# Two pads of 8 bytes in a partition, one ahead of the weight ring and one behind the arena

## The chip, the cores and the metric

The kernel runs on one core of one Trainium2 chip. The metric is the time on the device in microseconds for one execution. The kernel before takes 3476.79 us, the median of three runs (3474.61 to 3479.54).

## What is computed

Two stacks of two layers each work on one sequence of 256 tokens of width 1024, all in float32. The first stack has, in each layer, a feed-forward, a mixer and a feed-forward; the mixer is a bidirectional state-space mixer in layer 0 and multi-head latent attention in layer 1. The second stack has a recurrent mixer with pooling and a feed-forward that picks 16 of 16,384 experts per head. Nearly all of the time goes to matrix products with weights:

```python
h = modulate(x, norm_g[i, 0], mod[:, 0, 0], mod[:, 0, 1])
x = x + FFN_RES_WEIGHT * mod[:, 0, 2][:, None, :] * swiglu(h, w_gate, w_up, w_down)
...
act = jax.nn.gelu(jnp.einsum('td,ted->te', hx, u_sel), approximate=False)
return jnp.einsum('te,ted->td', gx * act, v_sel)
```

The kernel computes the expert layer densely: it multiplies with all rows of `peer_u` and `peer_v` and weights the result with gates that are zero for the experts that were not picked.

## The kernel before

**Tiling.** Activations stand transposed, 128 features in the partitions and 256 tokens in the free dimension. Weights come from memory as 957 blocks of 128 x 1024 float32 (512 KB, 4,096 bytes in each partition), in the order in which they are used. A block is used as eight 128x128 stationary operands.

**Weights in two parts.** For most stages each block is split. ScalarE rounds it into one of the four slots of `weights_hi` (`split_hi`, L1146), VectorE subtracts that from the block and writes the rest (`split_lo`, L1641), and TensorE makes three matmuls for each 128x128 piece: rounded weights with the rounded and with the remaining part of the activations, and the rest of the weights with the rounded part of the activations. `columns_in_parts` (L517) does this for a product that streams all eight feature tiles of `hh` and `h` (24 matmuls into one region of PSUM). `rows_in_parts` (L550) does it for a product that streams one tile, whose rounded part is in `small` and whose rest is in `work` (three matmuls into each of eight regions). `front` (L529, L530, L543) does it for the first three blocks of a stage. L504 opens accumulators with 512-column matmuls of zeros. L896 makes 128x128 float32 transposes.

**Where data stands.** The blocks go to a ring of 4 slots (`ring`) and, in some stages, to 8 more slots inside the arena, whose rest part is written in place under the name `more_lo`. The arena is 128 KB in a partition; every stage lays its own temporaries in it. Modulation weights go from a queue of GpSimd to four further places of the arena and are multiplied and summed there by VectorE (L1569). The experts' activations go to memory from `small` (`rs`, `rv`) and come back to `work`.

**Odd offsets in the arena before.** The convolution of the state-space mixer (L1699) adds four shifted copies: step by step it writes `o[:, to]` with `to` from element 2, 1, 0 and 0 on, so 8, 4, 0 and 0 bytes past the tile's start; the first and the last have 254 elements, the middle two 255. In the recurrent mixer four rows of ZPAD are 257 elements apart, and L1870 reads `z[:, 1:257]` of row `p % 4`, which begins 4, 8, 12 and 0 bytes past a multiple of 16 for p = 0, 1, 2, 3.

**Order.** SyncE issues the blocks' transfers, each waiting until the block that last used its slot was used (`block_used`). TensorE waits for `block_lo`, VectorE for `block_hi`, ScalarE for the transfer and for the slot of `weights_hi`.

**Addresses.** The tensors are allocated one behind the other in a partition. The program of the kernel before has them at these bytes: `ring` 16,512; `weights_hi` 32,896; `arena` 49,280, with `more_lo` inside it at 80,000; `x` 180,352; `h` 188,544; `hh` 196,736; `vfirst` 204,928; `cols` 209,024 (2,648 bytes long); `kept` 211,680; `zeros` 213,728; `eps` 213,984 (80 bytes long); `modc` 214,080; `one_minus_k_a` 215,040; `work` 215,072 (its second half, with the rest part of the gated rows, 219,168); `small` 223,264. Four constants of 4 bytes or less stand ahead of the ring at 16,384, 16,416, 16,448 and 16,480. The partition has 229,376 bytes, and the last tensor ends at 228,640.

Of the kernel before, what the change touches and what calls it, by code (L numbers as in the profile page):

```python
# [16 lines left out]
P = 128  # L17
# [252 lines left out]
def build(nc, stream, mods, cols_d, consts_d, x_d, pos_d, wuq_d, wukv_d, cond_d, keys_d, pool_d, lora_d, gup_d, vup_d, acts_d, out_d):  # L270
    with ExitStack() as ctx:
        def sb(name, shape, dt=F32):
            return ctx.enter_context(nc.sbuf_tensor(name, shape, dt))
# [6 lines left out]
        def sb_twice(name, shape, parts):  # L280

            with nc.sbuf_tensor(name, shape, F32) as whole:
                pass
            return whole, [sb(f"{name}_{i}", p, dt) for i, (p, dt) in enumerate(parts)]

        ring, (ring_lo,) = sb_twice("ring", [P, RING, 1024], [([P, RING, 1024], F32R)])
        whi = sb("weights_hi", [P, WS, 1024], F32R)
        with nc.sbuf_tensor("arena", [P, 128, 256], F32) as AR:
# [1 line left out]
        sb("arena_low", [P, 30, 256])  # L290
        more_lo = sb("more_lo", [P, MORE, 1024], F32R)
        sb("arena_high", [P, 128 - 30 - 4 * MORE, 256])
        x = sb("x", [P, DT, T])

        h, (h_lo,) = sb_twice("h", [P, DT, T], [([P, DT, T], F32R)])
# [2118 lines left out]
```

## Time and profile before

| | |
|---|---|
| median of three runs | 3476.79 us (3474.61 to 3479.54) |
| span of the profiled execution | 3476.7 us |
| TensorE matmul busy / weight load busy | 96% / 92% |
| VectorE, ScalarE, GpSimd busy | 74%, 46%, 6% |
| TensorE's granted clock, mean | 0.987 of 2.4 GHz |
| DMA engines, mean busy share | 58%, 203 GB/s |

The page gives the busy time of each engine, the chain of work that ended last and the costliest groups of instructions. A group line names the source line, the engine, what is written from what, the shapes and the count; then the busy time and the mean of one in ns; then the idle time of the engine before them and what ended it. Matmuls overlap in the array, so the mean of one (some 280 ns) is a latency; how often one starts is read from pieces of the chain or from the timeline.

### The profile page before, as it was taken

To read this page: it belongs to the slowest core of one execution; us is meant where nothing else is said; L and a number is where in the kernel's file an instruction comes from. 1 tells how busy PE (TensorE), PEld (TensorE's weight loads), DVE (VectorE), ACT (ScalarE), POOL (GpSimd) and SP (SyncE) were. 2 spreads that over 40 slices of the span, in tenths; PEclk is the share of its full clock that TensorE was granted. 3 is DMA by queue.
4 is the path that set the end of the run, shared out by engine and by line. 5 is a ranking of instruction groups with operands and counts; after the bars stand their busy time and mean duration, and the time that the engine had idled before them with its cause. 6 is when DMAs were issued, how large, how long until landed. Compare 5 with 4: busy or idle time off the path is not lost.

```text
span 3476.7 us, 68787 instructions
## 1 busy us (share of the span) xinstructions
PE 3342.0 (96%) x26804; PEld 3203.1 (92%) x26804; DVE 2579.5 (74%) x4576; ACT 1608.5 (46%) x2594; POOL 198.7 (6%) x331
## 2 busy tenths in 40 slices
PE   6999989999999998999999999999899999999998
PEld 5999869999967998889999999998789999999998
DVE  7889667888736896746977867776755977777776
ACT  3456644454445445134444444444414445444444
POOL 1100001101000220200000000000300000000000
PEclk9999999999999999999999999999999999999999
DMA  9964218979613993034664466665215665456665
GB/s 369 359 221 169 74 49 324 336 261 334 249 46 113 385 374 127 31 132 171 228 207 169 166 225 229 230 229 174 75 46 171 230 221 175 169 203 229 232 228 181
DMA packets 246578, 707.46 MB, mean 203 GB/s; under 512 B 27472, under 2 KB 93008, under 8 KB 244928
## 3 DMA queue, kind: packets, MB, share of 16 engines
q1 hardware_dynamic: 212112, 571.64, 47.2%
q0 software_dynamic: 34224, 132.46, 10.2%
q8 instruction: 167, 2.74, 0.3%
q14 instruction: 75, 0.61, 0.1%
HBM read 669.40 MB, written 34.60 MB: 202 GB/s over the span
## 4 chain that ended last, share of the span: by engine, by line
PE 85%; DVE 7%; DMA 4%; ACT 2%; issue 2%; SPq 0%; POOL 0%; DVEq 0%; ACTq 0%; POOLq 0%
PE psum L517 39%; PE psum L550 26%; PE psum L1074 3%; DMA ring<-stream 2%; PE psum L896 2%; PE psum L1009 1%; PE psum L647 1%; DVE ring L1641 1%; PE psum L916 1%; PE psum L498 1%; PE psum L529 1%; DMA arena<-mod_weights 1%; PE psum L530 1%; DVE arena L1569 1%; ACT weights_hi L1146 1%
## 5 line engine op out<-in xcount | busy, mean ns | idle before, releaser
L517 PE MATMUL psum<-hh,weights_hi 128*128 128x256 f32 x4216 | 1212.2, 288 | 19.2 <-ACT arena L1360 8.1
L1146 ACT ACTIVATE weights_hi<-ring 128x1024 fp32r<-128x1024 f32 x711 | 752.0, 1058 | 993.6 <-DMA ring<-stream 928.6
L517 PE MATMUL psum<-h,weights_hi 128*128 128x256 f32 x4216 | 1197.5, 284 | 0.0
L1641 DVE TENSOR_TENSOR ring<-ring,weights_hi 128x1024 fp32r<-128x1024 f32 x711 | 870.1, 1226 | 440.0 <-ACT weights_hi L1146 434.9
L517 PE MATMUL psum<-hh,ring 128*128 128x256 f32 x2976 | 845.5, 284 | 0.0
L517 PEld LDWEIGHTS psum<-hh,weights_hi 128*128 128x128 f32 x4216 | 814.2, 193 | 26.8 <-issue 11.3
L517 PEld LDWEIGHTS psum<-h,weights_hi 128*128 128x128 f32 x4216 | 814.1, 193 | 0.3
L550 PE MATMUL psum<-small,weights_hi 128*128 128x256 f32 x2752 | 774.5, 281 | 4.9 <-DVE work L1665 3.3
L550 PE MATMUL psum<-work,weights_hi 128*128 128x256 f32 x2752 | 772.1, 281 | 0.0
L550 PE MATMUL psum<-small,ring 128*128 128x256 f32 x2304 | 646.1, 280 | 0.0
L517 PEld LDWEIGHTS psum<-hh,ring 128*128 128x128 f32 x2976 | 574.9, 193 | 0.0
L550 PEld LDWEIGHTS psum<-small,weights_hi 128*128 128x128 f32 x2752 | 518.9, 189 | 7.6 <-issue 5.3
L550 PEld LDWEIGHTS psum<-work,weights_hi 128*128 128x128 f32 x2752 | 519.0, 189 | 0.0
L550 PEld LDWEIGHTS psum<-small,ring 128*128 128x128 f32 x2304 | 434.0, 188 | 0.0
L517 PE MATMUL psum<-hh,more_lo 128*128 128x256 f32 x1240 | 351.5, 283 | 0.0
L1641 DVE TENSOR_TENSOR more_lo<-arena,weights_hi 128x1024 fp32r<-128x1024 f32 x214 | 261.1, 1223 | 75.2 <-ACT weights_hi L1146 72.3
L1569 DVE SCALAR_TENSOR_TENSOR arena<-arena 128x1024 f32<-128x1024 f32 x232 | 281.7, 1219 | 11.4 <-DMA arena<-mod_weights 11.1
L1146 ACT ACTIVATE weights_hi<-arena 128x1024 fp32r<-128x1024 f32 x214 | 225.0, 1053 | 114.3 <-PE psum L517 87.0
L517 PEld LDWEIGHTS psum<-hh,more_lo 128*128 128x128 f32 x1240 | 238.7, 193 | 0.0
L2101 DVE TENSOR_SCALAR work<-kept,small 128x128 f32<-128x128 f32 x512 | 142.6, 342 | 83.0 <-PE psum L1074 77.5
L2112 DVE TENSOR_TENSOR work<-work,arena 128x256 f32<-128x256 f32 x256 | 159.1, 623 | 0.0
L2183 POOL DMA_DIRECT2D arena<-mod_weights x208 | 109.8, 528 | 575.8 <-DVE arena L1569 572.3
(410 smaller groups left out, 3897.0 us busy)
## 6 DMA issues: line engine op xcount, KB each, us to landing
ring<-stream SPq DMA_DIRECT2D x735, 512.0 KB, 3.6
arena<-mod_weights POOLq DMA_DIRECT2D x224, 512.0 KB, 6.3
arena<-stream SPq DMA_DIRECT2D x222, 512.0 KB, 5.7
acts<-small SPq DMA_DIRECT2D x256, 128.0 KB, 2.2
work<-acts SPq DMA_DIRECT2D x256, 128.0 KB, 2.2
arena<-cond_rows POOLq DMA_DIRECT2D x3, 1024.0 KB, 7.6
arena<-w_uq POOLq DMA_DIRECT2D x1, 3072.0 KB, 10.3
arena<-constants POOLq DMA_DIRECT2D x2, 1200.0 KB, 5.7
```

The lines of the kernel that those rows point to most:

```text
L498: mm = pe.matmul(PS[:, 2, 0:T], ones, SQ[:, d, :], start=(d == 0), stop=(d == DT - 1))
L517: mm = pe.matmul(out, lhs[:, d, :], rhs[:, d, :], start=(d == 0 and p == 0), stop=(d == DT - 1 and p == 2))
L529: pe.matmul(out, w[:, d, :], h_hi[:, d, :], start=opens and d == 0, stop=False, skip_group_check=True)
L550: mm = pe.matmul(acc[:, d, :], lhs[:, d, :], rhs, start=False, stop=False, skip_group_check=True)
L896: mm = pe.matmul(PS[:, (4 * st + b) % 8, j * P:(j + 1) * P], lhs[:, c, :], rhs[:, c, :], start=True, stop=True)
L1074: mm = pe.matmul(PS[:, 4 + g % 4, j * P:(j + 1) * P], OHI[:, g % 2, j, :], OHJ[:, g % 2, j, :], start=True, stop=True)
L1146: act.activation(whi[:, NTH[n] % WS, :], raw(n), ACT.Copy).then_inc(sem["block_hi"], 1)
L1569: return dve.scalar_tensor_tensor(PRODUCT[:, m % 2, :], block, 1.0, COND[:, 0 if g < 6 else 1, :], ALU.mult, ALU.mult, accum_out=modc[:, g ...
L1641: dve.tensor_tensor(low(n), raw(n), whi[:, NTH[n] % WS, :].bitcast(F32), ALU.subtract)\
L2101: dve.tensor_scalar(OHI[:, g % 2, j, :], iota, ijg[:, 0, t:t + 1], ijg[:, 2, t:t + 1], ALU.is_equal, ALU.mult)
L2112: dve.tensor_tensor(gat[:, k % 4, :], sil[:, k % 4, :], WALL[:, :, i * 4 + k], ALU.mult).then_inc(sem["pe_gated"], 1)
L2183: pool.dma_start(MODRING[slot], mods[i * MOD_RING + (first + slot + MOD_RING)]).then_inc(mod_full[slot], 16)
```

## The change

Two tensors are allocated that nothing reads or writes: `line_half`, 8 bytes in a partition, ahead of the ring, and `line_rest`, 8 bytes, between the arena and `x`. The description of the change is that weight ring, rounded weights and arena begin 8 bytes past a multiple of 16 in a partition and everything else is where it was, modulo 16. No instruction is changed but for the addresses of its operands.

```diff
@@ -283,6 +283,7 @@
                 pass
             return whole, [sb(f"{name}_{i}", p, dt) for i, (p, dt) in enumerate(parts)]
 
+        sb("line_half", [P, 2])
         ring, (ring_lo,) = sb_twice("ring", [P, RING, 1024], [([P, RING, 1024], F32R)])
         whi = sb("weights_hi", [P, WS, 1024], F32R)
         with nc.sbuf_tensor("arena", [P, 128, 256], F32) as AR:
@@ -290,6 +291,7 @@
         sb("arena_low", [P, 30, 256])
         more_lo = sb("more_lo", [P, MORE, 1024], F32R)
         sb("arena_high", [P, 128 - 30 - 4 * MORE, 256])
+        sb("line_rest", [P, 2])
         x = sb("x", [P, DT, T])
 
         h, (h_lo,) = sb_twice("h", [P, DT, T], [([P, DT, T], F32R)])
```

## Rows read from the trace of the kernel before

**Rows 1.** The page: busy us, share of the span, instructions.

```profile
PE 3342.0 (96%) x26804; PEld 3203.1 (92%) x26804; DVE 2579.5 (74%) x4576; ACT 1608.5 (46%) x2594; POOL 198.7 (6%) x331
```

**Rows 2.** The page: shares of the chain that ended last.

```profile
PE 85%; DVE 7%; DMA 4%; ACT 2%; issue 2%; SPq 0%; POOL 0%; DVEq 0%; ACTq 0%; POOLq 0%
```

**Rows 3.** The chain in order of time: start us, us, what, count.

```profile
53.06 118.08 PE psum L517 x984
171.14 59.15 PE psum L550 x504
...
1430.26 28.85 PE psum L896 x256
...
2025.70 356.23 PE psum L550 x3000
```

**Rows 4.** L504: timeline (start us, us), then duration ns min/median/max.

```profile
236.87 0.81 PE L504 MATMUL psum<-zeros 128*128 128x512 bf16 x3
...
L504 PE MATMUL psum<-zeros x168: 379/379/631, 37.6 to 3096.5; 128*128 128x512 bf16 x168
```

**Rows 5.** Stretches: busy us of each engine (count), TensorE clock, DMA share.

```profile
53.00:171.00 118.00, 118.00 (x986) 118.00 (x985) 105.54 (x151) 51.34 (x66) 21.11 (x40) 1.00 0.96 358
594.00:679.00 85.00, 85.00 (x710) 85.00 (x710) 70.42 (x98) 35.44 (x46) 12.82 (x25) 1.00 0.94 334
782.00:870.00 88.00, 88.00 (x736) 88.00 (x735) 72.28 (x101) 36.36 (x46) 13.73 (x26) 1.00 0.95 334
1130.00:1230.00 100.00, 93.90 (x759) 92.68 (x759) 88.50 (x129) 40.56 (x51) 20.59 (x39) 0.98 0.99 386
```

**Rows 6.** L1699: durations ns min/median/max, then its two shapes apart.

```profile
L1699 DVE SCALAR_TENSOR_TENSOR arena<-psum,cols,arena x128: 473/482/486, 251.8 to 382.7; 128x254 f32<-128x254 f32 x64, 128x255 f32<-128x255 f32 x64
...
L1699 DVE SCALAR_TENSOR_TENSOR arena<-psum,cols,arena 128x255 f32<-128x255 f32 x64 | 30.9, 483 | 2.3
L1699 DVE SCALAR_TENSOR_TENSOR arena<-psum,cols,arena 128x254 f32<-128x254 f32 x64 | 30.7, 480 | 8.7 <-ACT arena L1207 7.5
```

**Rows 7.** VectorE's timeline, L1870 for p = 0 to 3.

```profile
1341.30 0.48 DVE L1870 SCALAR_TENSOR_TENSOR arena<-arena,cols 128x256 f32<-128x256 f32 x1
...
1346.58 0.48 DVE L1870 SCALAR_TENSOR_TENSOR arena<-arena,cols 128x256 f32<-128x256 f32 x1
...
1349.56 0.48 DVE L1870 SCALAR_TENSOR_TENSOR arena<-arena,cols 128x256 f32<-128x256 f32 x1
...
1353.36 0.49 DVE L1870 SCALAR_TENSOR_TENSOR arena<-arena,cols 128x256 f32<-128x256 f32 x1
```

**Rows 8.** Groups by line and shape: busy us, mean ns, idle before.

```profile
L517 PE MATMUL psum<-hh,weights_hi 128*128 128x256 f32 x4216 | 1212.2, 288 | 19.2 <-ACT arena L1360 8.1 <-DVE arena L1674 6.4 <-DVE ring L1641 3.8
...
L1641 DVE TENSOR_TENSOR ring<-ring,weights_hi 128x1024 fp32r<-128x1024 f32 x711 | 870.1, 1226 | 440.0 <-ACT weights_hi L1146 434.9
...
L517 PE MATMUL psum<-hh,ring 128*128 128x256 f32 x2976 | 845.5, 284 | 0.0
...
L550 PE MATMUL psum<-small,weights_hi 128*128 128x256 f32 x2752 | 774.5, 281 | 4.9 <-DVE work L1665 3.3 <-DVE ring L1641 1.1 <-DVE work L2116 0.4
...
L1146 ACT ACTIVATE weights_hi<-ring 128x1024 fp32r<-128x1024 f32 x711 | 752.0, 1058 | 993.6 <-DMA ring<-stream 928.6 <-PE psum L517 46.8 <-PE psum L550 17.6
...
L517 PE MATMUL psum<-hh,more_lo 128*128 128x256 f32 x1240 | 351.5, 283 | 0.0
```

**Rows 9.** TensorE's timeline, a front's first matmuls, first and last of nine.

```profile
242.04 0.28 PE L530 MATMUL psum<-hh,ring 128*128 128x256 f32 x1
...
242.99 0.28 PE L530 MATMUL psum<-hh,ring 128*128 128x256 f32 x1
```

**Rows 10.** The page, DMA issues: count, KB each, median us to landing.

```profile
ring<-stream SPq DMA_DIRECT2D x735, 512.0 KB, 3.6
arena<-mod_weights POOLq DMA_DIRECT2D x224, 512.0 KB, 6.3
arena<-stream SPq DMA_DIRECT2D x222, 512.0 KB, 5.7
acts<-small SPq DMA_DIRECT2D x256, 128.0 KB, 2.2
work<-acts SPq DMA_DIRECT2D x256, 128.0 KB, 2.2
```

## The prediction

> **What bounds the kernel now.** I read the page first [rows 1]: TensorE is busy 96% of the span, its weight loads 92%, VectorE 74%. The chain that ended last [rows 2] agrees: 85% of it is TensorE, 7% VectorE, 4% waits for DMAs, which is 4% x 3476.7 = 139 us. L517 and L550 carry 39% and 26% of the span. So the first question is what sets the pace of those matmuls, and the second which other unit has little slack beside them.
>
> The pace is read from long unbroken pieces of the chain [rows 3]: 984 matmuls of L517 in 118.08 us are 120.0 ns each, 504 of L550 in 59.15 us are 117.4 ns, 3000 of L550 in 356.23 us are 118.7 ns. Neither of the two reads that a matmul makes of the state buffer needs that long. The moving side: three 512-column matmuls of L504 take 0.81 us from first start to last end, and one alone 379 ns, so they start (0.81 - 0.38) / 2 = 0.215 us apart, or 108 ns for 256 columns [rows 4]. The weights side: 256 pairs of a 128x128 load and a matmul of L896 follow each other in 28.85 us, 112.7 ns a pair [rows 3]. So at 120.0 ns there are 12 ns of cover over the moving read and 7.3 ns over the load, and something else sets the pace.
>
> Slack elsewhere [rows 5]: between 53 and 171 us VectorE is busy 105.5 of 118.0 us and the DMA engines 96%; in three other stretches DMA is at 94, 95 and 99%. DMA is the unit nearest to its limit.
>
> **The change part by part.**
>
> *The pads.* Two tensors of 8 bytes in a partition, which no instruction names: no instruction, DMA or wait is added or moved, on any queue. 0 us.
>
> *Where the tensors go.* The addresses of the kernel before stand above, and each is a multiple of 32 although `cols` (2,648 bytes) and `eps` (80 bytes) are not whole multiples: the tensor behind each was put at the next multiple of 32. An 8-byte `line_half` is then followed by a ring at 16,512 + 32 = 16,544, not at 16,520. I expect ring, `weights_hi` and arena 32 bytes further and everything behind the arena 64 bytes further. The half-line offset of the description would then not exist. I hold this at 0.96; both readings are costed below.
>
> *Engines, if the offset really is 8 bytes.* The kernel before already has such operands in the arena. The convolution's four steps (L1699) write 254 or 255 elements, starting 8, 4, 0 and 0 bytes past a multiple of 16. All 128 last between 473 and 486 ns, and the groups of 254 and of 255 elements, each half shifted, have means of 480 and 483 ns [rows 6]. L1870 reads its last operand at 4, 8, 12 and 0 bytes past one, since ZPAD's rows are 257 elements apart: 0.48, 0.48, 0.48 and 0.49 us [rows 7]. So VectorE pays nothing visible. For TensorE the trace has no shifted load. Its bound from above: a 512-byte operand that begins 8 bytes past a multiple of 16 touches 33 groups of 16 bytes in place of 32, and if the load takes time in proportion that is 1/32 of 112.7 ns = 3.5 ns, under the 7.3 ns of cover. So 0 us with the cover. If the cover were not there, 3.5 ns x 20,904 matmuls (3 x 4216 of L517 and 3 x 2752 of L550 [rows 8]) = +73 us. A gain I exclude here, as a shifted read touches no fewer groups. ScalarE's split (1058 ns a block, 46% busy) waits mostly for its DMA [rows 8], so a per cent on it is hidden.
>
> The Trainium skill ("SBUF — State Buffer", Specifications) speaks against the change: 16-byte lines, at least two hits on a line for full bandwidth, and a penalty for each crossing. With 4-byte words, 8 bytes past a multiple of 16 still gives every line at least two hits, so by the first half of the rule the sum stays at 0, and by the second it gets at most the extra crossing just costed. On VectorE the rows agree with the first half.
>
> *Engines, with a shift of 32 and 64 bytes.* What can differ is how the two reads of a matmul lie to each other. Before, all weights (ring, `weights_hi`, low parts) and `h`/`hh` begin at multiples of 64, while the gated rows in `work` and `small`, which only L550 streams, begin 32 past one. L517 runs at 120.0 and L550 at 117.4 to 118.7 ns. After, the weights begin 32 past a multiple of 64 and the moving operands stay as they were. I cost this at 0, because L529 and L530, whose operands lie to each other as L517's do, start nine matmuls at the head of a run within 0.95 us, 118.8 ns apart [rows 9], so the addresses alone do not fix 120.0; its ends are the two paces themselves, priced in the first rival.
>
> *DMA.* 957 blocks of 512 KB go to ring and arena, and 224 blocks of modulation weights [rows 10]. Their rows of 4,096 bytes keep their length and start at another multiple of 32. The trace shows no pair of transfers that differ only in that. Bound from below 0 (I see no way for a less round start to gain), from above the second rival. I take 0, since the 1,024-byte rows into `work`, 32 past a multiple of 64, land in the same 2.2 us as those out of `small` to memory [rows 10].
>
> The Trainium skill ("DMA: Bandwidth & Descriptors", How a descriptor splits into AXI transactions) says that a transfer fetches from the 256-byte boundary below its start. Ring rows start 128 past such a boundary before and 160 after, so a row would take 133 beats for 132. As an estimate from that page, the 139 us of DMA in the chain would grow by about 1 us. No row here shows it.
>
> *Sum.* 0 on the profiled 3476.7 us span. The median of the runs is 3476.79 and they lie between 3474.61 and 3479.54, so profile and runs agree within 0.1 us, and I forecast 3476.8.
>
> **The rivals.**
>
> *Faster: pace follows the lie of the two reads.* If a difference of 32 bytes (modulo 64) gives L550's pace and no difference gives 120.0, the change swaps them. L517: 12,648 matmuls x 2.6 ns = -33 us. L550: 2,112 in the feed-forwards (4 x 22 blocks x 24) x 2.6 + 6,144 in the value stages (2 x 128 blocks x 24) x 1.3 = +13 us. Net -20 us, 3457 us. For it: every long run of L517 is at 120.0 exactly and no run of L550 is. Against it: [rows 9], and L550 also differs in that it streams two tiles again and again and moves to other accumulator columns every third matmul. Chance 0.05.
>
> *Slower: writes that begin 32 bytes past a multiple of 64 take longer.* Place: the stretches where DMA is at 94% or more. It decides from about 4% on, the slack between 53 and 171 us. At 8%, the 139 us in the chain give +11; 53 to 171 would need 0.96 x 1.08 = 1.04 of its time (+4), and the stretches at 594 and 782 us 1.015 and 1.026 of theirs (+1, +2). Together +18, 3495 us. For it: DMA is the tightest unit. Against it: the transfers into `work` above, which begin so already, land as soon as those to memory. Chance 0.06, with smaller prices in the range.
>
> *Slower: the offset is real and the load has no cover.* The 73 us above, 3550 us. It needs both the allocation to put the ring at 16,520 and the load to be what sets 120.0 ns, which L896's 112.7 ns denies. Chance 0.02.
>
> *The change does not do what it says.* That is my reading, and it costs what the offset costs: nothing, 3476.8. Both forms of no change together have 0.85; 0.02 is left for causes that I do not see, split evenly.
>
> **How the numbers follow.** The likeliest case gives 3476.8. A measurement of this kernel can tell about 0.2%, 7 us, from no change. Faster 0.05 + 0.01 = 0.06, within 0.85, slower 0.06 + 0.02 + 0.01 = 0.09. The range takes the scatter of the runs (3474.6 to 3479.5), some microseconds below for a part of the first rival, and above for a DMA cost of up to 3%, under the slack (139 x 0.03 = 4 us): 3470 to 3485.
>
> **What would show it.** After the change the chain's long pieces should read 120.0 ns (L517) and 117.4 and 118.7 ns (L550), L1146 1058 ns, L1641 1226 ns, blocks landing in 3.6 and 5.7 us. The first rival would show L517 near 117.4 and L550 near 120. The second would show longer landing times, a DMA share at 1.00 between 53 and 171 us with TensorE idle behind L1641, and unchanged paces. The third would show L517 above 120.0 ns. The forecast is wrong at the root if the two long paces move at all; my reading of the addresses is wrong if the program puts the ring at 16,520.

## The result, and the profile after

The changed kernel takes 3438.07 us (median of four runs, 3435.34 to 3443.55) against 3478.12 for the kernel before (median of four): a ratio of 0.9887, 95% interval 0.9873 to 0.9902. (Here and below the ratios come from all the single runs, so they are not exactly the quotients of the medians.) That is 40 us faster, outside the range of the forecast. In its program `ring` begins at byte 16,544, `weights_hi` at 32,928, the arena at 49,312, `h` at 188,608, `hh` at 196,800, `work` at 215,136 and `small` at 223,328. So no tensor begins 8 bytes past a multiple of 16: the weights moved by 32 bytes and everything behind the arena by 64.

Two lines were added, so L517 is L519 here, L550 is L552, L1641 is L1643, L1146 is L1148. The page after (busy us, share, instructions; then the shares of the chain that ended last):

```profile
PE 3285.2 (96%) x26804; PEld 3142.9 (91%) x26804; DVE 2585.1 (75%) x4576; ACT 1608.5 (47%) x2594; POOL 196.6 (6%) x331
...
PE 76%; DMA 9%; DVE 8%; ACT 3%; issue 3%; SPq 0%; DVEq 0%; POOL 0%; POOLq 0%; ACTq 0%
```

Beside [rows 1] TensorE is busy 56.8 us less (3342.0 to 3285.2) with the same 26,804 matmuls, and its idle time, span less busy, grew by 15.7 us (134.7 of 3476.7 us before, 150.4 of 3435.6 after). The difference of the two is that of the spans, 41.1 us. VectorE and ScalarE are busy as long as before. Beside [rows 2] DMA's share of the chain went from 4% to 9%: where TensorE is faster, the transfers are more often what ends last.

The long pieces of the chain (start us, us, what, count), beside [rows 3]:

```profile
52.54 114.80 PE psum L519 x984
167.34 57.15 PE psum L552 x504
...
2094.03 122.91 PE psum L552 x1056
```

The first is 116.7 ns a matmul for 120.0, the second 113.4 for 117.4, the third 116.4 for 118.7. This third piece, of a value stage, is no pace of its own. Two windows in it without a stop (columns as in [rows 5]):

```profile
2095.00:2139.00 44.00, 44.00 (x376) 44.00 (x375) 33.26 (x48) 21.24 (x31) 0.00 (x0) 1.00 0.70 230
2152.00:2196.00 44.00, 44.00 (x391) 44.00 (x390) 33.81 (x49) 21.85 (x32) 0.00 (x0) 1.00 0.75 241
```

A window also counts the matmuls that are still in flight at its start (one lasts 0.28 us), so these are 44.28 / 376 = 117.8 ns and 44.28 / 391 = 113.2 ns. The same instructions with the same tiles ran first at the one pace and, after a short stop, at the other. Everything else that carries the time stayed as it was:

```profile
L1148 ACT ACTIVATE weights_hi<-ring 128x1024 fp32r<-128x1024 f32 x711 | 752.7, 1059 | 971.9 <-DMA ring<-stream 912.1
L1643 DVE TENSOR_TENSOR ring<-ring,weights_hi 128x1024 fp32r<-128x1024 f32 x711 | 870.2, 1226 | 414.5 <-ACT weights_hi L1148 411.3
...
ring<-stream SPq DMA_DIRECT2D x735, 512.0 KB, 3.8
...
arena<-stream SPq DMA_DIRECT2D x222, 512.0 KB, 6.1
```

1059 and 1226 ns are the values of [rows 8]. Four of the five kinds of transfers land 0.2 to 0.6 us later than in [rows 10] (those of the modulation weights 6.9 us for 6.3, those back into `work` 2.8 for 2.2), without more bytes. In the same first feed-forward as in [rows 5] the engines are asked for more in the same time:

```profile
53.00:171.00 118.00, 118.00 (x1015) 118.00 (x1014) 108.61 (x155) 53.09 (x70) 21.64 (x41) 1.00 0.98 369
```

1015 matmuls are counted in 118 us for 986, with TensorE's granted clock at 1.00 both times, so the clock is not the cause, and the DMA share is 0.98 for 0.96. The question is why a move by 32 and 64 bytes speeds up the matmuls.

### The profile page after: what moved, and what is told of

It is laid out like the page before. It is cut to its first block, busy times and chain, and to the rows that moved or that the text cites. A ratio compares the mean times of both kernels' runs of the same rounds, so it can differ in the third digit from the quotient of the medians.

```text
span 3435.6 us, 68787 instructions
## 1 busy us (share of the span) xinstructions
PE 3285.2 (96%) x26804; PEld 3142.9 (91%) x26804; DVE 2585.1 (75%) x4576; ACT 1608.5 (47%) x2594; POOL 196.6 (6%) x331
## 4 chain that ended last, share of the span: by engine, by line
PE 76%; DMA 9%; DVE 8%; ACT 3%; issue 3%; SPq 0%; DVEq 0%; POOL 0%; POOLq 0%; ACTq 0%
PE psum L519 33%; PE psum L552 24%; DMA ring<-stream 6%; PE psum L1076 3%; DMA arena<-mod_weights 3%; PE psum L898 2%; DVE ring L1643 1%; PE psum L1011 1%; PE psum L649 1%; ACT weights_hi L1148 1%; PE psum L918 1%; PE psum L500 1%; DVE arena L1571 1%; PE psum L531 1%; PE psum L532 1%
## 5 line engine op out<-in xcount | busy, mean ns | idle before, releaser
L519 PE MATMUL psum<-hh,weights_hi 128*128 128x256 f32 x4216 | 1201.5, 285 | 29.9 <-DVE arena L1676 9.7
L1148 ACT ACTIVATE weights_hi<-ring 128x1024 fp32r<-128x1024 f32 x711 | 752.7, 1059 | 971.9 <-DMA ring<-stream 912.1
L519 PE MATMUL psum<-h,weights_hi 128*128 128x256 f32 x4216 | 1183.4, 281 | 0.0
L1643 DVE TENSOR_TENSOR ring<-ring,weights_hi 128x1024 fp32r<-128x1024 f32 x711 | 870.2, 1226 | 414.5 <-ACT weights_hi L1148 411.3
L519 PEld LDWEIGHTS psum<-hh,weights_hi 128*128 128x128 f32 x4216 | 798.8, 189 | 39.7 <-DVE ring L1643 14.0
L519 PE MATMUL psum<-hh,ring 128*128 128x256 f32 x2976 | 834.9, 281 | 0.0
L519 PEld LDWEIGHTS psum<-h,weights_hi 128*128 128x128 f32 x4216 | 799.1, 190 | 0.2
L552 PE MATMUL psum<-small,weights_hi 128*128 128x256 f32 x2752 | 767.8, 279 | 9.2 <-DVE work L1667 5.8
L552 PE MATMUL psum<-work,weights_hi 128*128 128x256 f32 x2752 | 763.7, 277 | 0.0
L552 PE MATMUL psum<-small,ring 128*128 128x256 f32 x2304 | 639.5, 278 | 0.0
L519 PEld LDWEIGHTS psum<-hh,ring 128*128 128x128 f32 x2976 | 564.6, 190 | 0.0
L552 PEld LDWEIGHTS psum<-small,weights_hi 128*128 128x128 f32 x2752 | 518.1, 188 | 14.2 <-issue 8.3
L552 PEld LDWEIGHTS psum<-work,weights_hi 128*128 128x128 f32 x2752 | 517.1, 188 | 0.1
L552 PEld LDWEIGHTS psum<-small,ring 128*128 128x128 f32 x2304 | 433.7, 188 | 0.0
L519 PE MATMUL psum<-hh,more_lo 128*128 128x256 f32 x1240 | 346.6, 279 | 0.0
L1643 DVE TENSOR_TENSOR more_lo<-arena,weights_hi 128x1024 fp32r<-128x1024 f32 x214 | 261.0, 1223 | 63.8 <-ACT weights_hi L1148 63.3
L1148 ACT ACTIVATE weights_hi<-arena 128x1024 fp32r<-128x1024 f32 x214 | 225.1, 1054 | 112.1 <-PE psum L519 86.0
L519 PEld LDWEIGHTS psum<-hh,more_lo 128*128 128x128 f32 x1240 | 233.8, 189 | 0.0
```

Source lines behind the costliest of these rows:

```text
L519: mm = pe.matmul(out, lhs[:, d, :], rhs[:, d, :], start=(d == 0 and p == 0), stop=(d == DT - 1 and p == 2))
L552: mm = pe.matmul(acc[:, d, :], lhs[:, d, :], rhs, start=False, stop=False, skip_group_check=True)
L1148: act.activation(whi[:, NTH[n] % WS, :], raw(n), ACT.Copy).then_inc(sem["block_hi"], 1)
L1643: dve.tensor_tensor(low(n), raw(n), whi[:, NTH[n] % WS, :].bitcast(F32), ALU.subtract)\
```

## Experiments

Below, **distance** is the byte at which a streamed tile begins less the byte at which the weights begin, modulo 512. It is the same for all eight pieces of a block, since weights step by 512 bytes and streamed tiles by 1,024, and the same for ring, `weights_hi` and `more_lo`. *First products* are those of L517 (`h` and `hh` streamed), *second products* those of L550 (`small` and `work` streamed). Before, the distances were 0 and 416. After the change they are 32 and 448.

### Which addresses count: all, or one side

Everything 32 bytes further (e1):

```diff
+        sb("pad_front", [P, 8])
         ring, (ring_lo,) = sb_twice("ring", [P, RING, 1024], [([P, RING, 1024], F32R)])
```

> A pad of 32 bytes ahead of the ring only: every tensor of the kernel moves by 32 bytes, so weights and moving operands keep their distance. Theory A (the pace hangs on the distance between what a matmul streams and the weights, modulo 128): the paces of before, 120.0 ns (first products) and 117.4 ns (second products of the feed-forwards), time 3478 us. Theory B (the weights' own start, 32 past a multiple of 64, is what is fast): the paces of the changed kernel, 116.7 and 113.4 ns, 3438 us. Theory C (the moving operands' own start, modulo 128): neither pace is as before, something between 3438 and 3478 us.

Only what stands behind the arena, 32 bytes further (e2):

```diff
+        sb("pad_mid", [P, 8])
         x = sb("x", [P, DT, T])
```

> A pad of 32 bytes between the arena and x only: the weights stay at multiples of 64, everything behind the arena moves by 32. Distances are those of the changed kernel. Theory A: 116.7 and 113.4 ns, 3438 us. Theory B: the paces and the time of before, 120.0 and 117.4 ns, 3478 us. Theory C: the moving operands start where they do in the kernel moved by 32 bytes as a whole, so the same paces as in that one.

The same with 64 bytes, `sb("pad_mid", [P, 16])` (e3):

> A pad of 64 bytes between the arena and x only: the moving operands are at the addresses of the changed kernel, the weights at those of before. Theory A: h and hh now lie 64 past the weights (modulo 128), the place at which the second products ran at 113.4 ns, so first products near 113.4 ns; the gated rows lie 96 past them, not seen so far, between 113.4 and 120 ns; time 3415 to 3440 us. Theory B: time of before, 3478 us. Theory C: time and paces of the changed kernel, 116.7 and 113.4 ns, 3438 us.

Measured, with the pace of the first and of the second products of the feed-forwards, from the long pieces of each chain. The line "before" of each table was measured together with the runs below it:

| | distances | paces, ns | us | ratio to before (95%) |
|---|---|---|---|---|
| before | 0, 416 | 120.0, 117.4 | 3475.87 | |
| e1 | 0, 416 | 120.0, 117.4 | 3477.83 | 1.0002 (0.9992 to 1.0012) |
| e2 | 32, 448 | 116.7 or 117.8, 113.4 | 3434.67 | 0.9890 (0.9873 to 0.9907) |
| e3 | 64, 480 | 117.8, 118.4 | 3456.68 | 0.9943 (0.9926 to 0.9959) |

e1, then e2 (start us, us, what, count):

```profile
52.75 118.08 PE psum L518 x984
170.83 59.15 PE psum L551 x504
```

```profile
52.52 115.89 PE psum L518 x984
168.41 57.15 PE psum L551 x504
...
746.80 114.80 PE psum L518 x984
```

e1 has the weights where the changed kernel has them and is as slow as before; e2 has them where the kernel before has them and is as fast as the changed one. So the weights' own start (theory B) is out. e1 and e2 have `h`, `hh`, `work` and `small` at the same bytes and differ by 43 us, so the streamed tiles' own start (theory C) is out too. What is common to before and e1, and to the changed kernel and e2, is the distance. e3 also shows that the gain does not grow with it. Its first products were expected near 113.4 ns and took 117.8, and its time was expected at 3415 to 3440 us and was 3456.68: that size was not foreseen.

### The offset of the description, really made

With `align_bytes=8` ring, `weights_hi` and arena begin at 16,520, 32,904 and 49,288, and everything behind is moved by 16 bytes:

```diff
+        sb("line_half", [P, 2])
+        ring, (ring_lo,) = sb_twice("ring", [P, RING, 1024], [([P, RING, 1024], F32R)], 8)
+        whi = sb("weights_hi", [P, WS, 1024], F32R, 8)
...
+        sb("line_rest", [P, 2], F32, 8)
+        x = sb("x", [P, DT, T], F32, 16)
```

> The offset that the change is described with, really made: ring, rounded weights and arena begin 8 bytes past a multiple of 16, everything behind them is moved by 16 bytes. Theory A: the distance grows by 8 bytes in place of 32, so little is gained: 119 to 120 ns, 3468 to 3478 us, if the offset itself costs nothing. Theory B: no prediction beyond the time of before, 3478 us. The third rival of the prediction (a load begun in mid-line has no cover): first products above 120 ns, up to 3550 us.

3479.66 us, ratio 1.0009 (0.9999 to 1.0019): no gain, 1.7 us above the range expected, and no loss that the runs can tell. In the diff the lines in between are cut; the other tensors of these two groups are aligned in the same way. The distances are 8 and 424, the first products ran at 120.0 ns and the second of the feed-forwards at 118.4 (59.65 us for 504). A load that begins 8 bytes past a multiple of 16 costs TensorE nothing that this shows. VectorE's split of a block took 1228 ns for 1226, ScalarE's 1061 for 1058.

### Each half alone, and the way back

Only the gated rows, `sb("pad_gates", [P, 8])` ahead of `work` (e6); only the first products' tiles, 32 bytes ahead of `x` and 480 more ahead of `work` (e7); 96 bytes ahead of `x` (e8).

> A pad of 32 bytes ahead of work only: weights, x, h and hh stay, the gated rows of the second products get the distance that they have in the changed kernel (448). Theory A: first products at 120.0 ns, second of the feed-forwards at 113.4; 2112 x 4.0 = 8 us saved there, in the value stages up to 6144 x 4 = 25 us where VectorE and the DMA keep up: 3445 to 3468 us. Theory B: time of before, 3476 us.

> The other half: x, h and hh 32 bytes further, work and small 512 bytes further, so that only the streamed operands of the first products change their distance (32), the gated rows keep 416. Theory A: first products at 116.7 ns (in some runs 117.8), second at 117.4; 12648 x 3.3 = 42 us less what waits give back: 3440 to 3455 us. Theory B: time of before, 3476 us.

> Everything behind the arena 96 bytes further: distance 96 for the first products, 0 for the second. Theory A with 0 as the worst distance whatever the order of the matmuls: second products at 120.0 ns, slower than before there (2112 x 2.6 = 6 us, 6144 x 1.3 = 8 us), first products not seen at 96 before, between 113 and 120. The time is 3476 + 14 less up to 12648 x 6 ns = 76, so 3415 to 3490 us; the two paces are what tells. Theory B: time of before, 3476 us.

| | distances | paces, ns | us | ratio to before (95%) |
|---|---|---|---|---|
| before | 0, 416 | 120.0, 117.4 | 3478.44 | |
| e6 | 0, 448 | 120.0, 113.4 | 3461.85 | 0.9957 (0.9940 to 0.9973) |
| e7 | 32, 416 | 116.7, 117.4 or 118.7 | 3451.15 | 0.9927 (0.9910 to 0.9943) |
| e8 | 96, 0 | 120.0, 120.0 | 3494.36 | 1.0048 (1.0031 to 1.0065) |

e8 is the test in the other direction (start us, us, what, count):

```profile
52.78 118.08 PE psum L518 x984
170.86 60.49 PE psum L551 x504
...
2031.18 360.36 PE psum L551 x3000
```

Each pace follows its own distance, and the two savings, 17 and 27 us, add up to 44 us, beside the 40 that the change brought. In e7 the second products of one feed-forward took 59.15 us for 504 (117.4 ns) and those of the next 59.83 (118.7 ns), at the same distance of 416. 118.7 ns is also the pace of the value stages before [rows 3], at 416 too, which the prediction had priced as belonging to the stage. e8 has the first products at 96 as slow as at 0, and takes from the second what the kernel before still had: 14 us were expected for that, and it is 16 us slower, 4 us over the end of the wide range.

### TensorE alone

Three benches leave out the whole kernel. They copy `x` about and then let TensorE run stretches of 168 matmuls in the kernel's order, one distance after the other, with every other engine idle (TensorE's granted clock is 0.999 to 1.0). The loop, with the distance given by its name:

```python
for n in range(168):
    pe.matmul(PS[:, n // 24 % 2, 0:T], (W, W, WL)[n % 3][:, n // 3 % 8, :],
              tile((hi, lo, hi)[n % 3], distance // 4, n // 3 % 8), ...)
```

> No part of the kernel: a bench in which TensorE alone works, on data copied from x, so its output is not the reference's. 21 distances (0 to 512 bytes, modulo 512, between the start of the streamed operands and that of the weights), at each 168 matmuls in the order of the first products (streamed tile advances) and 168 in that of the second (two tiles streamed again and again, eight accumulator regions). Theory A, in the form that TensorE's two reads disturb each other: the pace changes with the distance here too, 120 ns at 0 and 8 in the first form, near 116.7 at 32, near 117.8 at 64; in the second form 117.4 at 416 and 113.4 at 448; 512 as 0. Theory D (what the distance changes is how TensorE's reads meet the reads and writes of ScalarE and VectorE): one pace at all distances.

The pieces of its chain for distances 64 and 96, first form (start us, us, what, count):

```profile
254.26 19.04 PE psum L85 x168
...
292.34 20.15 PE psum L88 x168
```

19.04 / 168 is 113.3 ns, 20.15 is 119.9. The others are read alike: 20.16 us or 120.0 ns at distance 0 (second form; the first contains the bench's start), 19.60 or 116.7 at 16, 19.88 or 118.3 at 48. Both forms ran at the same pace at every distance. So neither VectorE nor ScalarE nor a DMA takes part (theory D is out): with TensorE alone the pace hangs on where its two operands lie to each other. Which form a stretch has, eight accumulator regions or one, does not matter.

The second bench put the tiles at the kernel's own places, then close together, then moved both sides or only the weights (e9):

> A second bench of TensorE alone on data copied from x (its output is not the reference's). The first bench repeated with period 256 bytes but 32 bytes displaced against the kernel: 113.3 ns at 160 and 416 there, 113.4 ns at 448 in the kernel. Here the weights stand at the kernel's own places (32,896 and 80,000) and the streamed operands at the kernel's (distance 0 to 256), then everything close together with the weights at 0 and at 128 modulo 512, then with both sides shifted, then with the weights shifted alone. If the places decide: the kernel's paces in the first group (120.0 at 0 and 8, 116.7 or 117.8 at 32, 117.8 at 64, 120.0 at 96; 117.4 at 416, 113.4 at 448). If something else in the kernel displaces the curve (its waits, its other engines): the first bench's paces in all groups (116.7 at 8, 118.3 at 32, 113.3 at 160). Theory A, distance alone: 120.0 ns whenever both sides are shifted alike, and the weights shifted by 96 gives what the streamed side gives at 160 or 416.

One sentence of that expectation rests on a slip of mine: I had read the first bench's table one stretch off, and its curve is not displaced against the kernel. Read rightly the first bench already had 113.3 ns at 64, 192 and 448. The second bench agreed with it at these distances but for 192 (117.8): at the kernel's places 120.0 at 0 and 8, 116.7 at 32, 113.3 at 64 (where e3 had 117.8), 119.9 at 96; second form 117.3 at 416, 113.4 at 448; the same close together, with the weights at 0 and at 128 modulo 512. Both sides moved alike by 8, 32, 64 or 160 bytes: 119.9 to 120.0 ns each time. Weights moved alone by 64: 113.5 ns, by 160: 119.9. It is the distance, in either direction.

All stretches of the benches and the feed-forwards of the kernels together, ns a matmul:

| distance | pace | distance | pace |
|---|---|---|---|
| 0, 256 | 120.0 | 96, 352 | 120.0 |
| 8 | 120.0 | 128, 384 | 118.6 |
| 16 | 116.7 | 160, 416 | 117.3 or 118.7 |
| 24 | 120.0 | 192, 448 | 113.3 or 117.8 |
| 32, 288 | 116.7 or 117.8 | 224, 480 | 118.3 |
| 48 | 118.3 | 504 | 115.5 |
| 64, 320 | 113.3 or 117.8 | 424 | 118.4 (e4) or 119.9 (e9) |

The curve repeats after 256 bytes. At some distances it has two values, and the third bench asked which of them is taken (e11):

> A third bench of TensorE alone at the kernel's places (its output is not the reference's). In the first two benches some distances showed two paces: 64 bytes 113.3 (bench) and 117.8 ns (kernel), 192 bytes 113.3 and 117.8, 32 bytes 116.7 and 117.8, 160 bytes 117.3 and 118.7; and 0, 96 and 256 only 120.0. Here the same distances are reached after other distances and after a pause of some 1.5 us. If the way in which the two reads fall into step at the start of a stretch decides: at 32, 64, 160 and 192 both values turn up, one or the other, none in between, and at 0 and 96 always 120.0. If the distance alone decides, one value each. Four stretches give the distance 192 to only some of the pairs (one of the two weight tiles, or one of the two streamed tiles) and 0 to the rest: if each pair pays for itself, the paces lie between 113.3 and 120.0 in proportion to the pairs, about 115.6 ns with two of three matmuls at 192 and 117.8 with one of three; if one bad pair holds the others, 120.0.

Distance 64 behind a stretch at 0, then 64 behind a stretch at 48:

```profile
240.91 19.79 PE psum L90 x168
...
280.58 19.04 PE psum L92 x168
```

117.8 and 113.3 ns, at the same distance and addresses. Distance 32 gave 117.8 behind 0 and 116.7 behind 24 and behind a pause. So with the addresses fixed, what ran just before (the distance there, or a pause) goes with one of two steps, and none in between appeared. It is not the distance of the stretch before alone: 192 behind 160 was 113.4 ns here and 117.8 in the second bench, where the stretch at 160 itself had run at its other pace. 192 gave 113.3 to 113.5 every time here (behind a pause, 0, 160 and 448). 0 and 96 were always at 120. The four stretches with 192 for only some of the pairs took 20.07 to 20.09 us; less the 0.28 us that a start behind a pause adds at distance 0 (20.43 for 20.15), all ran at 117.8 ns, whether one or two of three matmuls had it: neither in proportion (115.6) nor held by the worst (120.0). Both forms of my expectation were wrong there.

### A version that beats both

```diff
+        sb("pad_mid", [P, 48])
         x = sb("x", [P, DT, T])
...
+        sb("pad_gates", [P, 24])
         work, (_, gat_lo) = sb_twice("work", [P, 2048], ...
```

> A kernel meant to be faster than both: 192 bytes between the arena and x, 96 more ahead of work, so that both the first and the second products have a distance of 192 modulo 256, the one at which the second products ran at 113.4 ns. Theory A with a period of 256 bytes: first and second products at 113.4 ns; against the changed kernel 12648 x 3.3 = 42 us less of matmul time, of which waits for VectorE and the DMA give a good part back: 3395 to 3435 us. If the period does not hold in the kernel: a first pace other than 113.4 ns and a time between 3435 and 3490 us.

3411.19 us for 3481.68, ratio 0.9813 (0.9784 to 0.9842); with the changed kernel at 0.9887 (0.9873 to 0.9902) the intervals lie apart. The time is in the range expected, and both paces of the feed-forwards are those expected:

```profile
PE 3252.5 (96%) x26804; PEld 3108.2 (91%) x26804; DVE 2583.4 (76%) x4576; ACT 1608.0 (47%) x2594; POOL 196.6 (6%) x331
```

```profile
52.40 111.52 PE psum L519 x984
163.92 57.13 PE psum L552 x504
```

113.3 and 113.4 ns in the two products of the feed-forwards. In the value stages the second products did not keep 113.4: the two long pieces of the first one are 1440 matmuls in 168.64 us and 1344 in 157.84, 117.1 and 117.4 ns, close to the other pace of this distance. TensorE is busy 89.5 us less than in [rows 1]; 15.5 us of that came back as idle time (3402.7 - 3252.5 = 150.2). The profiled run is the fastest of the four (3404.39 us); they reach up to 3428.91, a scatter of 25 us. The four runs of e8, whose two distances have shown one pace only, lie within 3 us. That the scatter comes from the choice between two paces fits this, but is not shown.

## Why the prediction was wrong

**The addresses.** Right: ring at 16,544, weights moved by 32 and the rest by 64, no half-line offset. And the rows on the shifted VectorE operands [rows 6, 7] pointed the right way: e4, with the offset really there, costs nothing that its ten runs can tell.

**"I cost this at 0, ... so the addresses alone do not fix 120.0".** This is the step that failed: the term for a shift of 32 and 64 bytes was put at 0, and the change measured -40 us. [rows 9] shows nine matmuls at the head of a run, just behind a wait, 118.8 ns apart. I took that as the same operands running at another pace. The same run, followed further, says otherwise:

```profile
246.11 0.28 PE L530 MATMUL psum<-hh,ring 128*128 128x256 f32 x1
```

From the last line of [rows 9] (242.99) to this one there are 26 more starts in 3.12 us: 120.0 ns each. The head of a run is a transient, and behind it these operands have the pace of L517, 984 matmuls in 118.08 us [rows 3]. So [rows 9] was no evidence against the addresses; the benches show that a distance has one or two steady paces, and at 0 only 120.0. What the runs showed in place of the 0 is that the distance between the streamed tile and the weights sets the pace: 120.0 to 116.7 ns for 0 to 32, 117.4 to 113.4 for 416 to 448. The row that spoke loudest, first products at exactly 120.0 ns in every long run and second ones never, I had in hand and gave 0.05.

**The size of the first rival.** Its mechanism, pace from the lie of the two reads, is what the runs show; its law was wrong. I gave it 0.05 and forecast the opposite, so that it stands there is no merit of the forecast. I let the pace depend on the distance modulo 64, so the second products had to get slower (+13 us) and the net was -20. The curve repeats after 256: 416 to 448 is 117.4 to 113.4, and I had read the 118.7 ns of the value stages as a matter of the stage, where it is the other pace of 416. By the measured paces the terms are 12,648 x 3.3 = -42 us, 2,112 x 4.0 = -8 us and, in the value stages, 6,144 x 2.3 (118.7 to 116.4) = -14 us. That is 64 us, against 56.8 us less busy time on the page. 15.7 us came back as idle time, for which the rival's sum had no term.

**Cover.** "12 ns of cover over the moving read and 7.3 ns over the load, and something else sets the pace" took the two reads one by one. Each alone does fit. Together, at distance 0, they do not run at 113.3, and it is this that sets the pace. The Trainium skill ("TensorE: Matmul & The Clock Gate", Part 2) says of TensorE's two read ports that "Loading the next tile's weights doesn't steal SBUF read bandwidth from the running matmul." Taken literally this does not fit the benches: with TensorE alone, up to 6.7 ns of 120 go with where the two operands lie to each other, and the measurement decides. Which part of TensorE or of the memory makes it so, they do not show.

**DMA.** The second rival did not occur as such: the landing times rose a little (3.6 to 3.8 us, 5.7 to 6.1), but that goes with the faster TensorE and not with the start of the writes. e1, with ring and arena 32 bytes past their old places, has 3.5 and 5.8 us and the time of before; e2, with ring and arena at their old places and the fast paces, has 3.8 and 6.1. The 1 us that I estimated from the Trainium skill ("DMA: Bandwidth & Descriptors", How a descriptor splits into AXI transactions) is too small for these runs to show. I had put it on rows that are written, where the rule tells of what a transfer fetches.

**What stays open.** Why the distance counts with a period of 256 bytes, what the two reads share, and what sets which of two steady paces a run takes. The steps 113.3, 116.7 and 120.0 ns are 272, 280 and 288 cycles at 2.4 GHz, a pattern that I can only report; 117.8 ns (282.7 cycles) does not fit it.

## What to carry to other kernels

If a kernel is bound by matmuls that load new weights each time, the pace of long unbroken runs should be read for each pair of tiles and compared; a difference of some per cent between equal shapes may be a matter of addresses, and a pad of a few dozen bytes in front of the streamed tensor tests it. A kernel whose layout shifts for any reason can move by that alone, here by +0.5% (e8) to -1.9% (e10), so comparisons of other changes should keep the places of the tensors. Where an allocator rounds, read the addresses in the program before reasoning about an offset.

## What was not expected of the hardware

Float32 matmuls of 256 columns, each with its own 128x128 load, ran at 113.3 to 120.0 ns with all other engines idle, depending on the distance between the two operands modulo 256 and, at some distances, on what ran before. An absolute shift of both operands, 8 bytes past a multiple of 16 included, changed nothing (119.9 to 120.0 ns at distance 0). At the faster distances a common shift of 8 bytes was not tried, so a cost that fits under the 6.7 ns between 113.3 and 120.0 would not have shown.
